# A gate table for 16384 experts: built by one-hot matrix products, or by accumulating scatters from GpSimd

## What is computed

```
scores = einsum('bshpc,hpkc->bshpk', q, sub_keys)        # 8 heads, 2 halves, 128 keys
half_vals, half_idx = top_k(scores, 16)                  # per half
cand_vals = half_vals[..., 0, :, None] + half_vals[..., 1, None, :]
top_vals, top_pos = top_k(cand_vals, 16)                 # per head, of 256
expert_idx = take_along_axis(cand_idx, top_pos)          # i1 * 128 + i2
gates = softmax(top_vals)
act = gelu(einsum('ted,td->te', U[expert_idx], x)) * gates
out = einsum('te,ted->td', act, V[expert_idx])
```

## Time and profile before

| | |
|---|---|
| median of three runs | 3787.35 us (3786.58 to 3788.13) |
| the profiled execution | 3787.0 us, its span 3785.3 us |
| TensorE busy | 3765.2 us, 99% |
| VectorE, ScalarE, GpSimd busy | 2884.2, 1429.7, 1489.6 us |
| moved by DMA | 740.38 MB |

### The profile page before, as it was taken

How to read it: one execution, slowest core, us unless ns; L and a number is a source line. 1 busy time by engine, 2 the same in 40 slices (tenths; PEclk the granted TensorE clock), 3 DMA queues, 4 the chain that set the end, 5 groups by cost and what they waited for, 6 DMA issues and landing times.

```text
span 3785.3 us, 53817 instructions
## 1 busy us (share of the span) xinstructions
PE 3765.2 (99%) x17262; PEld 3116.1 (82%) x17262; DVE 2884.2 (76%) x4108; ACT 1429.7 (38%) x1953; POOL 1489.6 (39%) x950
## 2 busy tenths in 40 slices
PE   9999999999999999999999999999999999999998
PEld 7788888888888888888877888888888888888887
DVE  7854659899998288788788555598999973887877
ACT  5533343333333333333455333333333333333334
POOL 1100004444444377666211000044444443776762
PEclk9999999999999999999999999999999999999999
DMA  3222224445554699999322223244455547999993
GB/s 124 83 95 100 101 84 142 142 177 193 193 190 167 217 360 372 364 354 344 133 74 83 100 100 103 82 148 143 171 197 191 191 168 240 366 374 360 351 336 112
DMA packets 325068, 740.38 MB, mean 196 GB/s; under 512 B 30640, under 2 KB 161840, under 8 KB 321584
## 3 DMA queue, kind: packets, MB, share of 16 engines
q1 hardware_dynamic: 105408, 381.73, 28.9%
q10 hardware_dynamic: 174448, 222.40, 17.1%
q0 software_dynamic: 45056, 134.38, 9.8%
HBM read 618.87 MB, written 119.54 MB: 195 GB/s over the span
## 4 chain that ended last, share of the span: by engine, by line
PE 95%; DVE 2%; issue 1%; ACT 1%; DMA 0%; ACTq 0%; POOL 0%; DVEq 0%; SPq 0%; POOLq 0%
PE banks L1370 64%; PE banks L1623 25%; PE banks L1600 2%; PE banks L1452 1%; PE banks L1547 1%; PE banks L1443 1%; PE banks L1466 0%; ACTq L738 0%; PE banks L1436 0%; ACT xh L503 0%; DMA vrow<-in_stream,tail_v 0%; DVE xl L872 0%; ACT hi L487 0%; DVE hT L1309 0%; DVE acc L1276 0%
## 5 line engine op out<-in xcount | busy, mean ns | idle before, releaser
L1370 PE MATMUL banks<-xh,hi 128*128 128x512 f32 x3264 | 1288.1, 395 | 0.5 <-DVE xl L872 0.5
L1370 PE MATMUL banks<-xl,hi 128*128 128x512 f32 x3264 | 1274.8, 391 | 0.0
L1370 PE MATMUL banks<-xh,lo 128*128 128x512 f32 x3264 | 1272.6, 390 | 0.0
L433 POOL TENSOR_TENSOR lo<-raw,hi 128x1024 fp32r<-128x1024 f32 x240 | 648.1, 2701 | 977.6 <-ACT hi L487 977.5
L860 DVE TENSOR_TENSOR lo<-raw,hi 128x1024 fp32r<-128x1024 f32 x482 | 582.9, 1211 | 380.9 <-ACT hi L487 379.8
L487 ACT ACTIVATE hi<-raw 128x1024 fp32r<-128x1024 f32 x724 | 738.8, 1043 | 268.4 <-DMA raw<-in_stream 163.5
L1370 PEld LDWEIGHTS banks<-xh,hi 128*128 128x128 f32 x3264 | 614.3, 188 | 132.2 <-issue 10.2
L1370 PEld LDWEIGHTS banks<-xh,lo 128*128 128x128 f32 x3264 | 613.5, 188 | 129.1
L1370 PEld LDWEIGHTS banks<-xl,hi 128*128 128x128 f32 x3264 | 614.4, 188 | 122.6 <-issue 5.3
L1623 PE MATMUL banks<-hi,ah 128*128 128x512 f32 x1536 | 473.5, 390 | 0.5 <-DVE al L1245 0.5
L1623 PE MATMUL banks<-lo,ah 128*128 128x512 f32 x1536 | 473.3, 390 | 0.0
(11 more groups left out here) (229 smaller groups left out, 3366.3 us busy)
## 6 DMA issues: line engine op xcount, KB each, us to landing
raw<-in_stream SPq DMA_DIRECT2D x724, 512.0 KB, 3.4
early<-eo ACTq DMA_DIRECT2D x256, 256.0 KB, 2.3
gate_table<-stage ACTq DMA_DIRECT2D x24, 2048.0 KB, 6.9
gb<-gate_table ACTq DMA_DIRECT2D x64, 768.0 KB, 10.4
eb<-early ACTq DMA_DIRECT2D x64, 768.0 KB, 15.8
vrow<-in_stream,tail_v POOLq DMA_INDIRECT x256, 7.8
hval<-early,tail_h POOLq DMA_INDIRECT x256, 7.3
hT<-in_xT ACTq DMA_DIRECT2D x4, 512.0 KB, 8.6
```

Source lines behind the costliest of these rows:

```text
L433: pool.tensor_tensor(lo[k % RING][:, :], raw[k % RAW][:, :], hi[k % RING][:, :].bitcast(f32), ALU.subtract).then_inc(lo_split, 1)
L1370: ins = pe.matmul(out_ap, st[slot][:, a:a + P], mv, start=first and i == 0, stop=last and i == 2)
```

## The change

The table's layout becomes `gate_table[i2][i1 * 384 + token]`. It is zeroed by twelve copies a layer from the zero tiles that stand at the end of the weight stream, issued by ScalarE, three in each of the four attention pairs (`clear`). Each slot's gate is then added to its cell by GpSimd: one accumulating indirect DMA per chunk and slot, with 128 tokens in each, 384 a layer (`scatter`). Since two heads of one token can pick the same expert, the 16 slots of a head are issued together and the next head of that chunk waits until they have landed. Chunk 0 runs first, alone; then the heads of the chunks 1 and 2 alternate. `select(c)` now ends with the cell's number for every slot (`place`, `scat_at`) in place of the transposes. GpSimd keeps the splits of the tiles 4 to 19; VectorE makes those of the tiles 20 to 67, one after each step of the selections 1 to 3 (`tick`), and all later ones. The transposes, one-hots, their products and the stores from `stage` are gone, and `select(3)` follows the others at once. ScalarE waits after tile 121 for the scatters to land.

```diff
-TURNS = ((12, 8), (12, 19), (10, 29))
-HOT_E, POOL_E, LAST_T = 36, 124, 116
+LAST_T = 116
+TICKS, TOP_TICK, EARLY_TOP = 16, 12, 10
+ZEROS = 3
...
+CUT = NK * M // (PAIRS * ZEROS)
...
-    gate_table = nc.dram_tensor("gate_table", (NTB, P, NK * TB), f32, kind="Internal").ap()
+    gate_table = nc.dram_tensor("gate_table", (P, NK * M), f32, kind="Internal").ap()
+    gate_cells = gate_table.rearrange("p (n o) -> (p n) o", o=1)
...
+                def scatter(c, h):
+
+                    if h:
+                        pool.wait_ge(scat_done[c], l * (SLOTS * 16) + h * (TOPK * 16))
+                    for j in range(h * TOPK, (h + 1) * TOPK):
+                        apart(pool)
+                        pool.indirect_dma_start(gate_cells, bass.IndirectOffsetOnAxis(scat_at[c][:, j:j + 1], 0),
+                                                scat_g[c][:, j:j + 1], None, compute_op=ALU.add).then_inc(scat_done[c], 16)
...
-                with pool.Fori(0, (POOL_E - AHEAD) // 8) as c:
+                with pool.Fori(0, TICKS // 8) as c:
                     for k in range(8):
                         split(N_U + AHEAD + k, c)
+
+                pool.wait_ge(zero_done, (l + 1) * (PAIRS * ZEROS * 16))
+                pool.wait_ge(picks_ready, l * MT + 1)
+                for h in range(PH):
+                    scatter(0, h)
+                pool.wait_ge(picks_ready, l * MT + 2)
+                scatter(1, 0)
+                pool.wait_ge(picks_ready, l * MT + 3)
+                scatter(2, 0)
+                for h in range(1, PH):
+                    scatter(1, h)
+                    scatter(2, h)
...
+            def clear(b, z):
+
+                act.dma_start(gate_table[:, bass.ds(b * (ZEROS * CUT) + z * CUT, CUT)].rearrange("p (a n) -> p a n", a=AHEAD),
+                              stream[DEPTH * T:DEPTH * T + AHEAD, :, :].rearrange("a p n -> p a n")).then_inc(zero_done, 16)
...
-                        for u in range(2):
-                            act.wait_ge(table_out[u], 16 + (l + 1) * (NTB * 8))
+                        for c in range(MT):
+                            act.wait_ge(scat_done[c], (l + 1) * (SLOTS * 16))
                         fetch(0, 0, 0)
                         fetch(1, 0, 1)
...
+                def tick(k):
+                    if k >= TICKS:
+                        split(l, N_U + AHEAD + k)
...
                     batch(HP, lambda j: dve.max(hv[:, j, 0:8], sc(j)))
+                    tick(k0)
                     batch(HP, lambda j: dve.max_index(hx[:, j, 0:8], hv[:, j, 0:8], sc(j)))
+                    tick(k0 + 1)
...
+                        link(dve.tensor_scalar(place[:, :, :], slot3[:, 0, :, :], float(M), tokcol[:, c:c + 1], ALU.mult, ALU.add))
+                        dve.scalar_tensor_tensor(flat(scat_at[c][:, :]), slot3[:, 1, :, :], float(NK * M), place[:, :, :],
+                                                 ALU.mult, ALU.add).then_inc(picks_ready, 1)
...
-                for n in range(QUADS):
-                    one_hots(n)
-                add_low(QUADS - 2)
-                add_low(QUADS - 1)
...
-                for at, turns in HOT_PARTS:
...
+                experts(0, 8)
+                with pe.Fori(0, NK // 8 - 1) as i:
+                    experts(8, 8, i)
```

More of the change, by code:

```diff
@@ L82 @@
 NVEC = C_QEPS + 1
[L84 to L100, removed]
+CUT = NK * M // (PAIRS * ZEROS)
+assert CUT == AHEAD * 1024 and TICKS * NBLK < LAST_T
+DVE_LAYER, DVE_PAIR, DVE_TURN = 219, 14, 2
 LOWEST = -3.0e38
@@ L214, in trunk_kernel @@
     SC = sb("SC", o_t, [P, NBLK, HP, NK])
-    tabs = sb("tabs", o_t + 32 * KB, [P, 2, M])
+    scat_at = [sb(f"scat_at{c}", o_t + 32 * KB + 512 * c, [P, SLOTS], u32) for c in range(MT)]
+    scat_g = [sb(f"scat_g{c}", o_t + 32 * KB + 512 * (MT + c), [P, SLOTS]) for c in range(MT)]
+    place = sb("place", o_r + 30 * KB, [P, PH, TOPK])
     S2 = sb("S2", o_r, [P, HP, NK])
@@ L310, in trunk_kernel @@
         keys_hi, keys_lo, qh_ready, scores_out, sc_ready = sem("keys_hi"), sem("keys_lo"), sem("qh_ready"), sem("scores_out"), sem("sc_ready")
[L311 to L316, removed]
+        top_ready, ex_ready, picks_ready = sem("top_ready"), sem("ex_ready"), sem("picks_ready")
+        zero_done, scat_done = sem("zero_done"), [sem(f"scat_done{c}") for c in range(MT)]
         gate_in = [sem("gate_in0"), sem("gate_in1")]
@@ L384, in _ @@
                                  allow_small_or_imprecise_dtypes=True))
+            steps.link(pool.iota(tokcol[:, :], [[P, MT]], base=0, channel_multiplier=1,
+                                 allow_small_or_imprecise_dtypes=True))
             for r in (0, DH):
@@ L590, in _ @@
                     split(l, 8, b)
+                    clear(b, 1)
                     weights(1)
@@ L702, in exponents @@
                     act.activation(ex[:, :, :], ex[:, :, :], ACT.Exp, scale=rsT[:, c:c + 1]).then_inc(ex_ready, 1)
[L704 to L719, removed]
-                    dense_gelu(N_U + e, even(e) if e < EARLY * EG else odd(e))
[L721 to L731, removed]
+                for e in range(LAST_T):
+                    dense_gelu(N_U + e, even(e) if e < EARLY * EG else odd(e))
+                    if e == EARLY_TOP:
+                        exponents(0)
+                    if e % TICKS == TOP_TICK + 1 and TICKS < e < NBLK * TICKS:
+                        exponents(e // TICKS)
                 def fetch(g, r, u):
-                    act.dma_start(gb[:, u, :, :],
-                                  gate_table[:, :, bass.ds(g * (EG * TB), EG * TB)].rearrange("b p n -> p b n"))\
+                    act.dma_start(gb[:, u, :, :], gate_table[:, bass.ds(g * (EG * M), EG * M)].rearrange("p (e t) -> p e t", t=M))\
                        .then_inc(gate_in[u], 16)
@@ L1176, in _, with flat @@
+                def flat(t):
+                    return t.rearrange("p (h k) -> p h k", k=TOPK)
                 dve.wait_ge(sc_ready, (l + 1) * HP)
                 apart(dve)
-                for c in range(MT):
+                select(0)
+                dve.wait_ge(lo_split, RAW + l * T + N_U + AHEAD + TICKS)
+                apart(dve)
+                for c in range(1, NBLK):
                     select(c)
-                take_tabs(MT - 1)
-                dve.wait_ge(gates_low, (l + 1) * MT)
@@ L1281, in period @@
                             low(g, 1 - z)
-                dve.wait_ge(lo_split, RAW + l * T + N_U + POOL_E)
-                apart(dve)
-                for e in range(POOL_E, NK + AHEAD):
+                for e in range(AHEAD + NBLK * TICKS, NK + AHEAD):
                     split(l, N_U + e)
@@ L1569, in experts @@
                         dense(l, N_U + k, bank[4 + k % 2][:, :], (xh, xl), i, (xl_ready, l * (4 * DC) + 2 * DC) if k == 0 else None)
-                def turn_slots(c):
-                    pe.wait_ge(slots_ready, l * MT + c + 1)
-                    for z in range(3):
-                        ins = pe.transpose(bank[6][:, z * P:(z + 1) * P], slot3[:, z, :, :].rearrange("p h k -> p (h k)"),
-                                           ident[:, :])
-                    ins.then_inc(turned, 1)
-                pe.wait_ge(sc_ready, (l + 1) * HP - 2)
```

107 lines of the change are left out of this document (24 added, 83 removed).

## The result

The changed kernel takes **4045.65 us** (median of 4 runs, 4044.97 to 4047.1) where the kernel before takes 3787.74 beside it: a ratio of 1.068, 95% interval 1.066 to 1.070. Forecast were 3694 us and a range up to 3960. The sign was wrong, and the rival with the right sign, (a) with 3956 us, was still 90 us short.

A forecast was written before the change was run, and what follows sets the result against it. TensorE was taken to bound the kernel: 3787.0 us less 97.0 for removed transposes and one-hot products, plus 0 for scatters and 4 for zeroing, gave 3694 us. The whole range was 3685 to 3960 us.

The forecast's parts named there:

- (a): Expert stage: an accumulating scatter costs GpSimd more than a gather, three fit per tile, TensorE stops; 3956 us, chance 0.32.
- What bounds the kernel: Whole kernel: TensorE, busy 3765.2 of 3785.3 us; other engines or queues count only if they make it stop.
- Part 1: Expert stage: all transposes and one-hot products leave TensorE, 48.5 us a layer, 97.0 us in all.
- Part 2: Expert stage: VectorE takes 48 splits a layer between top-k steps, and the later ones, at no cost.
- Part 3: Expert stage: GpSimd's 384 accumulating scatters a layer, 1.24 us each, end at 1237, before TensorE would stop: 0 us.
- deadline 1241: Layer 0's expert stage: TensorE stops if scatters land after 1241, because tile 124 needs the bank of GELU 122.
- gap 0.30: GpSimd in the expert stage: 0.30 us from one scatter to the next, taken from the gathers.
- Landings: First chunk's eight heads: each waits for its scatters to land, eight times 3.7 us, 29 us a layer.
- Meetings with VectorE: Expert stage: scatters beginning inside VectorE's two-input instructions are delayed, 54 us during the selections and 27 us after.
- three per tile: Expert stage: scatters between 1.06 and 1.51 us lock into three per tile, 1.81 us each, ending at 1372.
- the stretch beyond 1.51 us: Expert stage: accumulating scatters longer than 1.51 us, past three per tile; a tenth of the slower rival's 0.32 chance.
- Part 4: Mixing stage: ScalarE issues 24 zeroing copies of 2 MB, a third of 13 us on the path: 4 us.

The follow-up runs named there:

- the two chunks: The changed kernel scattering only chunks 0 and 1, 256 accumulating scatters a layer, the third chunk's gates left out: 3686.8 us.
- the plain run: The changed kernel with its 768 scatters as plain writes instead of accumulating ones: 3687.78 us.
- the last kernel: The changed kernel with plain scatters, duplicates summed on VectorE, and ScalarE's wait for the scatters after tile 122 instead of 121: 3689.51 us.

## Why the prediction was wrong

**What bounds the kernel: right.** TensorE's instructions set the time, and everything else counted only by making it stop. Two stops of together 354 us and the products slowed behind them, less the 100 us gained, are the 258 us.

**Part 1, 97.0 us off TensorE: right.** U is 696.4 us where 697.0 was computed. Against the 745.5 us of before that is 49.1 a layer, 98.2 in all. The run without the add is 99.9 us below before; the last 1.7 us I have not traced.

**Part 2, VectorE's splits for nothing: right.** In the changed kernel and its variants TensorE waited for a split (`lo`) for 0.3 us at most in a whole run, and the runs without a stall end at 3686 to 3690.

**Part 3 failed, in one term:** "I take 0.94, since 128 indices are what both gathers share with the scatter." It was 1.548. The number of indices is not what a gather and an accumulating scatter have to share; the gathers that I compared only moved data, and no row did an add. The gathers' rows say that the size of a piece doesn't matter, which says nothing on an operation. The frame around this term held: start at 656.9; deadline 1241; gap 0.30. With the true 0.96 of a plain scatter the last was built at 1229.0 and had landed by 1231.9, when ScalarE's first load of the table went out without a wait; the sum had 1237, and 1227 for the shorter landings. Two of the smaller terms were too large. Landings: in layer 0 the seven waits of chunk 0's heads came to 18 us, 2.6 each with the usual gap of 0.30 in them, where eight times 3.7 beyond it were taken. The Trainium skill (DMA: Bandwidth & Descriptors, Anatomy of one DMA) has 2.0 us fixed. The trace of the two chunks shows 2.9 at least and 3.4 in the median from issue to landing, 1.55 of them GpSimd's own time, between that figure and my 4.9. Meetings with VectorE: the plain run lost 64 us in layer 0 (431 us busy, less 384 x 0.955) against 54 + 27. Errors of 13 and 17 us had no weight beside 384 times 0.61 us.

**Rival (a) had the step and the sign, not the size.** That an accumulating scatter costs GpSimd more than a gather is what the runs show. That it does so because the destination is read as well, and that this falls to one of two cores, no run shows; 144 packets against 32 only say that more is moved. Its three per tile are there to be seen with 1.40 us. But its 1.81 us was worked out for scatters below 1.51, and beyond that nothing locks: 1.55 + 0.30 = 1.85 apart, from 656.9 on, with 24 us for meetings and 18 for landings, both as measured:

384 x 1.85 + 24 + 18 = 752, so the last is built by 1409. Three more gaps, of 1.7 to 2.9 us, that I have not traced make it 1413.6, and the table's first load goes out at 1415.2. TensorE stands 178 us in layer 0 and 176 in layer 1, by the trace. With the 99.9 gained and about 2 us a layer for the slower products after the stop, 3787.7 - 99.9 + 354 + 4 = 4046, the measured time. I gave the stretch beyond 1.51 us a chance of 0.03. That point lay 0.04 us below what came, and no row bounded the term from above but gathers disturbed by VectorE; with the rival's own reason, a read beside the write, the range should have gone up to an estimate of twice the gather's 0.94, 1.88 us.

**Part 4, zeroing: 0 instead of 4 us.** Issues took 592 ns at least and 743 at most; the mixing stage's rows are those of before. The 1338 ns of the earlier trace rows did not belong to ScalarE's issue as such, nor to the V stage: with the table in its new layout the same loads of `early` take 0.39 us in the median there, at 0.93 of the engines' time instead of 0.98, and the table's own 0.34. That it was the short runs of the old layout, queued before them, is likely and not shown.

## To carry to other kernels

An add inside a DMA was not free for the engine that builds it: before work is moved to GpSimd, find a row for the same operation, and where there is none, compute at which duration the schedule breaks and how far away that is. Here the margin was 0.12 us on a term taken 384 times a layer. The add on a gather, an edit of the kernel before that is one word and a zeroing, would have priced it before anything was built. Where an accumulate is only there for rare collisions, sum the collisions on an engine with time to spare and write plainly: that turned +258 us into -98.

## What the runs showed of the hardware

- GpSimd's time for one indirect DMA of 4-byte elements: 0.94 us gathering 128, 0.96 scattering, 1.55 accumulating scatter, 1.53 accumulating gather; with 64 indices 0.90 for the plain scatter and 1.40 for the adding one. To the next it is 0.30 us in every case.
- An accumulating scatter of 128 elements is 144 packets, with 64 elements 80, a plain one 32 for either. From 920 to 1230 its queue held 21.0% of the transfer engines' time for 0.09 MB, where that of the plain ones held 1.7% for 0.13 MB.
- A plain scatter that begins inside VectorE's subtraction (two inputs from SBUF, 1.23 us) ends 0.82 to 0.83 us after it, like the gather of the earlier trace rows.
- After a stop TensorE is slow for a while. The granted clock of the stall was 0.51, which is the level of 1.2 GHz; the first products after it are 0.43 us apart instead of 0.23, and the 96 that follow the stop took 23.8 us where four tiles take 21.8. The stop of 5.9 us was followed by such products too (granted clock 0.50), the stop of 0.9 us in the last kernel was not (1.00).
